# A two-block fp32 model on one core: ScalarE's order in the state-space chunks, the order of the first GLU units, and the place of one norm's sums

## The reference

```
# odd layer of the first block
hn = rmsnorm(h, norm_odd)                 # needs the sum of squares over 1024 features of each token
p  = hn @ w_in_odd                        # 1024 x 3072; 12 units of 128 columns "X", 12 units "G"

# state-space layer of the second block
u  = rmsnorm(h, norm_mix)                 # 512 x 1024, in 64 groups of 16 channels
x_t = A * x_(t-1) + B * u_t               # per group, 64 complex states
y  = gelu(Re(C x) + d * u)
ab = y @ w_glu                            # 1024 x 2048
h  = h + a * sigmoid(b)
```

## Time and profile before

| | us |
|---|---|
| median of the runs | 1719.63 |
| the profiled execution's own time | 1718.13 |
| its span | 1716.2 |
| PE busy | 1691.8 (99%) |
| DVE, ACT, POOL busy | 869.2, 762.9, 969.3 |

### The profile page before, as it was taken

One profiled execution on the slowest core, in us unless ns is written; L12 is line 12 of the kernel. 1 busy time (PEld: TensorE's weight loads), 2 busy tenths in 40 slices (PEclk: granted clock), 3 DMA queues, 4 the chain that ended last, 5 costly groups with the idle time before them and its releaser, 6 DMA issues.

```text
span 1716.2 us, 20954 instructions
## 1 busy us (share of the span) xinstructions
PE 1691.8 (99%) x8056; PEld 1396.0 (81%) x8056; DVE 869.2 (51%) x1250; ACT 762.9 (44%) x1203; POOL 969.3 (56%) x606
## 2 busy tenths in 40 slices
PE   9999999999999999999999999999999999999998
PEld 7888888777778898888888888888678888888887
DVE  3999997757787785522212121386644221212124
ACT  5333325466867773343222222454765332323234
POOL 5858755657678565654444444664547444444464
PEclk9999999999999999999999999999999999999999
DMA  4322323222245234222222222223112222222221
GB/s 170 105 99 87 111 99 115 95 74 95 89 162 211 68 128 136 99 91 95 97 98 99 98 98 98 86 98 99 47 47 93 98 99 98 98 92 95 97 99 62
DMA packets 56258, 172.65 MB, mean 101 GB/s; under 512 B 6496, under 2 KB 14816, under 8 KB 55264
## 3 DMA queue, kind: packets, MB, share of 16 engines
q1 hardware_dynamic: 56160, 171.33, 29.5%
HBM read 165.01 MB, written 6.29 MB: 100 GB/s over the span
## 4 chain that ended last, share of the span: by engine, by line
PE 70%; DVE 5%; ACT 3%; issue 2%; POOL 1%; DMA 1%; SPq 0%; DVEq 0%; ACTq 0%
PE B L315 57%; PE B L1687 1%; PE B L2439 1%; PE B L2441 1%; PE B L2437 1%; PE B L2235 1%; PE B L2335 1%; PE B L2314 1%; DVE SW L1150 1%; PE B L298 1%; DVE B L1016 1%; PE B L1614 1%; PE B L1579 1%; PE B L300 1%; PE B L299 1%
## 5 line engine op out<-in xcount | busy, mean ns | idle before, releaser
L291 POOL TENSOR_TENSOR WL<-RAW,WH 128x1024 fp32r<-128x1024 f32 x281 | 681.8, 2428 | 613.6 <-ACT WH L287 613.3
L287 ACT ACTIVATE WH<-RAW 128x1024 fp32r<-128x1024 f32 x281 | 296.5, 1057 | 627.3 <-PE B L315 593.8
L315 PE MATMUL B<-P0h,WH 128*128 128x512 f32 x1096 | 428.1, 391 | 3.7 <-ACT WH L287 1.9
L315 PE MATMUL B<-P0l,WH 128*128 128x512 f32 x1096 | 421.9, 390 | 1.3 <-DVE P0l L432 1.3
L315 PE MATMUL B<-P0h,WL 128*128 128x512 f32 x1096 | 276.4, 389 | 0.0
L315 PEld LDWEIGHTS B<-P0h,WH 128*128 128x128 f32 x1096 | 205.7, 188 | 48.4 <-DVE Yl L428 2.6
L315 PEld LDWEIGHTS B<-P0l,WH 128*128 128x128 f32 x1096 | 205.8, 188 | 44.4 <-DVE P0l L432 2.3
L315 PEld LDWEIGHTS B<-P0h,WL 128*128 128x128 f32 x1096 | 205.7, 188 | 42.7
L439 DVE TENSOR_TENSOR H<-H,B 128x512 f32<-128x512 f32 x88 | 60.2, 686 | 288.3 <-PE B L315 288.2
L1967 DVE SCALAR_TENSOR_TENSOR TMP<-B,RS 128x512 f32<-128x512 f32 x64 | 44.1, 691 | 258.5 <-PE B L315 244.1
L315 PE MATMUL B<-P1h,WH 128*128 128x512 f32 x448 | 174.7, 390 | 0.0
(11 more groups left out here) (354 smaller groups left out, 2668.8 us busy)
## 6 DMA issues: line engine op xcount, KB each, us to landing
RAW<-in_w SPq DMA_DIRECT2D x281, 512.0 KB, 3.2
PX<-in_zeros SPq DMA_DIRECT2D x4, 1024.0 KB, 10.0
H<-in_xT SPq DMA_DIRECT2D x8, 256.0 KB, 4.8
U<-u SPq DMA_DIRECT2D x32, 64.0 KB, 2.0
g<-GB SPq DMA_DIRECT2D x8, 256.0 KB, 2.1
GB<-g SPq DMA_DIRECT2D x32, 64.0 KB, 2.0
out<-Q SPq DMA_DIRECT2D x4, 512.0 KB, 3.6
CA<-in_zeros SPq DMA_DIRECT2D x1, 1920.0 KB, 10.0
```

Of the source, the lines that this page charges most:

```text
L287: act.activation(WH[:, i % NS, :], RAW[:, i % NR, :], ACT.Copy).then_inc(*inc("w_hi", i))
L291: pool.tensor_tensor(WL[:, i % NS, :], RAW[:, i % NR, :], WH[:, i % NS, :].bitcast(F32), ALU.subtract).then_inc(*inc("w_lo", i))
L315: return pe.matmul(b[:, :], w[:, ws[c]], x[:, c, :], start=start, stop=stop)
```

## The change

Three edits. In ScalarE's loop over the state-space chunks, `act_u` of chunk q+3 moves ahead of `act_g` of chunk q-2 and `act_gelu` of chunk q. In `pe_glu_start` the loop over chunks becomes the outer one and the loop over the three units the inner one; the waits for the banks and for `w_lo` of all three units stand ahead of the first matmul. In `pe_odd`, `stat_sums` moves from behind X0 to behind the second chunk of X1 (through the argument `between` of `linear`, L330).

```diff
--- before.py
+++ after.py
@@ -804,7 +804,8 @@
             i = IDX[what]
             wh, wl = weights(i)
             if kind in "XG":
-                linear(pe, what, P0h, P0l, range(8), ("x_lo", ("xc" if kind == "X" else "y", c)), "odd" if n == 0 else None)
+                linear(pe, what, P0h, P0l, range(8), ("x_lo", ("xc" if kind == "X" else "y", c)), "odd" if n == 0 else None,
+                       {1: lambda: stat_sums(pe, "odd", pool=rbanks)} if n == 1 else {})
             elif kind == "O":
                 if c == 0:
                     banks.queue.extend(rbanks.queue)
@@ -837,9 +838,7 @@
                     last.then_inc(*inc("unit", what if j else ("q4", 2 * c)))
                     if (c, j) == (3, 0):
                         pe_square_sums(pe, (4, 5))
-            if (kind, c) == ("X", 0):
-                stat_sums(pe, "odd", pool=rbanks)
-            elif (kind, c) == ("X", 1):
+            if (kind, c) == ("X", 1):
                 stat_spread(pe, "odd", pool=rbanks)
 
     def unit_key_ri(r, h):
@@ -1753,11 +1752,11 @@
         for q in range(8):
             if q < 7:
                 act_toeplitz(act, q + 1)
+            if q + 3 < 8:
+                act_u(act, q + 3)
             if q > 1:
                 act_g(act, q - 2)
             act_gelu(act, q)
-            if q + 3 < 8:
-                act_u(act, q + 3)
             if q + 2 < 8:
                 act_decay(act, q + 2)
             if q + 3 < 8:
@@ -1804,19 +1803,18 @@
     def pe_glu_start(pe, chunks):
 
         for what in GLU[:3]:
-            i = IDX[what]
-            wh, wl = weights(i)
             if chunks[0] == 0:
                 _, before = banks.take(what, "evac_a" if what[2] > 7 else "evac_d")
                 pe.wait_ge(*at(*before))
-                pe.wait_ge(*at("w_lo", i))
-            b = banks.bank[what]
-            for c in chunks:
-                pe.wait_ge(*at("g_lo7" if c == 7 else "g_lo", ("g", c)))
-                ws = slice(128 * c, 128 * c + 128)
-                last = mm3(pe, b[:, :], wh[:, ws], wl[:, ws], P0h[:, c, :], P0l[:, c, :], c == 0, c == 7)
-            if chunks[-1] == 7:
-                last.then_inc(*inc("unit", what))
+                pe.wait_ge(*at("w_lo", IDX[what]))
+        for c in chunks:
+            pe.wait_ge(*at("g_lo7" if c == 7 else "g_lo", ("g", c)))
+            ws = slice(128 * c, 128 * c + 128)
+            for what in GLU[:3]:
+                wh, wl = weights(IDX[what])
+                last = mm3(pe, banks.bank[what][:, :], wh[:, ws], wl[:, ws], P0h[:, c, :], P0l[:, c, :], c == 0, c == 7)
+                if c == 7:
+                    last.then_inc(*inc("unit", what))
 
     def pe_glu(pe):
         pe_glu_start(pe, range(7, 8))
```

## The result

| | before | changed |
|---|---|---|
| median, us | 1717.84 | 1725.88 |
| lowest to highest (5 runs each) | 1717.40 to 1719.90 | 1724.07 to 1726.78 |
| profiled execution | 1718.13 | 1724.07 |
| its span | 1716.2 | 1722.1 |

The ratio is 1.0040, with a 95% interval of 1.0030 to 1.0051: the change makes the kernel slower, by 0.4%. As a difference the forecast was +5.05 us; the ratio gives +6.9 us and the two medians +8.0.

A forecast was written before the change was run, and what follows sets the result against it. TensorE, busy 1691.8 of 1716.2 us, was taken as the bound, so anything that stops it is paid in full. -0.9 + 3.0 + 2.95 = +5.05 us on 1719.63 gave 1724.7 us, with 8 in 10 for 1720.5 to 1729.

The forecast's parts named there:

- The sums, -0.9: Odd layer: four matmuls of X1 ahead of the norm sums fill TensorE's gap, so X1 ends 0.9 us earlier.
- the root: GpSimd's root, needed by the spread behind X1, ends at 343.62, before X1's matmuls at about 345.3; not late.
- u, +3.0: Chunk loop: u ahead of g delays g by 1.0 us in each of three iterations; y of chunk 6 3.0 us later.
- the first stop: Some 2 us of u's 3.0 us loss was expected ahead of y of chunk 5, waiting for gelu of chunk 4.
- The GLU order, +2.95: First three GLU units: 4.4 us waiting for the third unit's weights, less 0.25 and 1.2 us given back.
- The stop: Behind y of chunk 6, TensorE waits 4.4 us for the low half of the third GLU unit's weights.
- Chunk 7: Second part of the GLU units: chunk 7's low half of g is ready with 0.7 us left, so not late.
- The clock, 0 in the sum: Behind the GLU wait: granted clock expected to read 1.00, costing nothing; bounded at up to +6.3 us.
- the rival with the falling clock: Clock falls to 1.2 GHz in the wait ahead of the GLU units: +3.1 us more, 1727.8 us; chance 0.20.
- The fast rival: Waits for DMA, chunk 6, weights and sums go and none comes: -3.55 us, 1716.1 us; chance 0.06.
- the rival with slack: Chunk loop: ScalarE's 2.21 us of waiting absorbs u; only the other edits count, +2.05, 1721.7 us; chance 0.15.
- the circle: Chunk loop: g on ScalarE releases GpSimd, whose tables ScalarE awaits before the next g; period 10.53 us, u lengthens it.

The follow-up runs named there:

- e1: Only u moved ahead of g and gelu on ScalarE, against the kernel before: median 1722.04 us against 1719.27, ratio 1.0016.
- e7: Changed kernel plus 17 matmuls of constants ahead of the wait for the GLU weights: median 1724.59 us, ratio 1.0032 to before.
- e2: Only the chunk-by-chunk order of the three GLU units with its waits ahead, against before: median 1723.64 us against 1719.27, ratio 1.0027.
- e8: Only the GLU order, each unit waiting for its own weights at its first matmul, against before: median 1722.05 us against 1719.28, ratio 1.0017.
- e10: The changed kernel measured again as it is, against before: median 1725.62 us against 1717.99, ratio 1.0039.
- e11: Changed kernel plus GpSimd's tables ahead of the low half of g: median 1720.31 us against 1717.99 of before, ratio 1.0010.
- e4: Kernel before with only chunks 3 to 6 of the three GLU units chunk by chunk: median 1718.11 us against 1719.27, ratio 0.9993.
- e3: Only the sums of squares moved into X1, against the kernel before: median 1718.40 us against 1719.27, ratio 0.9994.
- e5: Kernel before with GpSimd's tables of chunk q+3 ahead of the low half of g: median 1718.11 us against 1719.28, ratio 0.9994.
- e9: Before with sums inside X1, tables and u ahead of g, GLU chunks 3 to 6 chunk by chunk: median 1715.23 us against 1717.99, ratio 0.9979.
- e6: Kernel before with GpSimd's tables ahead of g's low half and u ahead of g on ScalarE: median 1717.48 us against 1719.28, ratio 0.9991.

## Why the prediction was right, and which term was off

- **The place.** What TensorE lost lies at the places named, in waits and in the slow clock behind the last of them, and the range and the direction held. That the forecast came within 1.2 us of the median is in part luck: it stood on a base of 1719.63 us, and the median of before was 1717.84 when five runs of it were counted, on the lower of two levels. By that base the same +5.05 us would have given 1722.9, 3.0 us too low, and 5.05 us (0.29%) lies just below the interval of the ratio.
- **The sums, -0.9.** Measured -0.92 (from sums to spread), with the root not late. Right in the trace; by the times alone it is not clear of the noise.
- **u, +3.0.** Measured +2.98 in e1 and +2.99 in the changed kernel. The steps were right too: g 11.5 us apart, y waiting for gelu. Only the place of the first stop was off: I put some 2 us of it ahead of y of chunk 5, waiting for gelu, and it stood one step earlier, ahead of T of chunk 6 (2.32 us, for ScalarE's copy of T of chunk 5), with 0.18 us left for y. The size is the same.
- **The GLU order, +2.95.** Without the low clock it is 29.99 - 27.16 = +2.83 (e7). The stop was put at 4.4 us and the start came 4.5 us later than before, and the second part gave back 1.32 us (11.73 to 10.41) where 1.2 was expected. Chunk 7 was not late.
- **The clock, 0 in the sum.** This is the term that was mis-sized. The step that took it as nothing in the likeliest case failed: the clock fell in or behind the stop in all five profiles that had it (changed, e2, e8, e10, e11), and behind the stop of 2.3 us for T in one of four (e10, not changed, e1 and e7). The price set for the rival was 3.1 us; one stretch costs 1.6 us, and 2.3 in e11. So the mechanism that came was that of the rival with the falling clock, at about half its price. With it the sum is -0.92 + 2.98 + 4.43 = +6.5 us, and the ratio gives +6.9 us. I had given this case 0.20, since no row that I showed of before had the lower level. The trace of before has it, though, at its very end, where TensorE's last matmul ends at 1709.36 us:

```profile
1712.00:1716.00 4.00, 0.00 (x0) 0.00 (x0) 0.00 (x0) 0.00 (x0) 0.00 (x0) 0.50 0.82 326
```

The clock is at 0.50 there after less than 3 us without a matmul, while the forecast stop was 4.4 us. That gives no price, but it speaks for a much higher chance. The rule of the Trainium skill ("TensorE: Matmul & The Clock Gate", section "Why this matters for your kernels"), which warns of long pauses between bursts of matmuls, was borne out: the clock stood at 0.50 behind a stop of 4.25 us, and behind the one of 2.7 us in e8 as well.

- **The fast rival and the rival with slack.** Both fell: the circle had no slack (e1), and the weights came 4 us behind y of chunk 6 in every version that waited for them.

## What to carry to other kernels

Before moving an instruction ahead of another, ask what the passed one releases, and follow it until it comes back to the same engine: 1.0 us of u was free in a wait and cost 3.0 us in the circle that made that wait, and reordering the other engine of the circle took 1.3 us off the distance and made the move harmless. When several units are interleaved, the first matmul waits for the latest weights of all of them; interleave only where all are surely there. On an engine that is 99% busy, count a stop of a few us with the slow clock behind it (here 1.6 to 2.3 us on top of 4.25), and look in the whole trace for a place where the clock is low before you put that cost at nothing.

## What the runs showed of the hardware

The low clock also comes without a long stop, and not in every execution. The 32 runs of the kernel before in the first set of experiments lie at 1717.5 to 1717.9 (9 runs), 1719.1 to 1719.9 (19) and 1720.2 to 1721.0 (4), steps of some 1.6 us. The traces show what a step is: e4 took 8.05 us from sums to spread where before took 6.43, which is 1.62 us. The profiled executions agree: those of e3, e5 and e9 have one such stretch and lie on the upper level of their kernel's runs (1718.40, 1718.05, 1715.23 us), those of e1 and e6 have none and lie on the lower (1720.72, 1715.77 us). In e4's profile it lies behind the sums in the odd layer (tiny matmuls, and a wait of 0.72 us ahead of them), as stretches:

```profile
340.00:341.00 1.00, 0.97 (x9) 1.00 (x9) 0.00 (x0) 0.47 (x1) 0.45 (x1) 1.00 0.83 336
...
342.00:343.00 1.00, 1.00 (x4) 0.81 (x3) 0.00 (x0) 0.00 (x0) 1.00 (x2) 0.50 0.00 0
```

And in e9's it lies near 550 us, behind the matmuls of 2 columns of the second block's norm (L1418 before), where TensorE had waited for only 0.28 us:

```profile
547.00:548.00 1.00, 1.00 (x10) 1.00 (x10) 1.00 (x1) 0.00 (x0) 1.00 (x1) 1.00 0.98 393
...
549.00:550.00 1.00, 1.00 (x3) 0.71 (x3) 1.00 (x3) 0.95 (x3) 1.00 (x2) 0.50 0.99 423
```

TensorE is counted busy in the first of these stretches, for most of it with matmuls of 2 columns, and the clock stands at 0.50 in the second. e3, e7, e10 and e11 show it at the same place as e9, and from the spread to y of chunk 0 these five take 235.0 us, against 233.4 in the others: 1.6 us. All five have the sums inside X1; of the six profiles with that edit only the first of the changed kernel is without it, and none of the seven without the edit has it. Two of those seven (e4, e5) have the stretch behind the sums instead, and none of the six. So the place where a stretch falls seems to go with the place of the sums, but no run here tests that, and why one execution has a stretch and another has not stays open. The edits of e3 and e4 are smaller than one such step, which is why their intervals hold 1 although their distances are clear.
